# The delta-rule products of the second mixer, issued on the two halves of the array's columns

## What is computed

```python
def gated_delta_rule(q, k, v, g, beta):
    ...
    lower = jnp.where(strict, jnp.einsum("bhnid,bhnjd->bhnij", k_beta, k) * decay, 0.0)
    t_inv = lax.linalg.triangular_solve(eye + lower, ...)
    u = jnp.einsum("bhnij,bhnjd->bhnid", t_inv, v_beta)
    w = jnp.einsum("bhnij,bhnjd->bhnid", t_inv, k_beta * jnp.exp(gc)[..., None])
    attn = jnp.where(tril, jnp.einsum("bhnid,bhnjd->bhnij", q, k) * decay, 0.0)
    def step(state, inp):
        v_new = u_i - jnp.einsum("bhcd,bhde->bhce", w_i, state)
        o = (jnp.einsum("bhcd,bhde->bhce", q_i * jnp.exp(g_i)[..., None], state)
             + jnp.einsum("bhij,bhje->bhie", a_i, v_new))
        state = state * jnp.exp(g_last)[..., None, None] + jnp.einsum("bhcd,bhce->bhde", k_dec, v_new)
        return state, o
```

## Time and profile before

| what | value |
|---|---|
| median of 3 runs | 1586.18 us |
| the profiled execution, its own time | 1586.05 us |
| its span in the trace | 1584.2 us |
| PE (matmul) busy | 1531.3 us, 97% |
| PEld (weight load) busy | 1437.0 us, 91% |
| DVE / ACT / POOL busy | 65% / 53% / 22% |
| DMA | 254.2 MB, mean 160 GB/s |

### The profile page before, as it was taken

One profiled execution on the slowest core, in us unless ns is written; L12 is line 12 of the kernel. 1 busy time (PEld: TensorE's weight loads), 2 busy tenths in 40 slices (PEclk: granted clock), 3 DMA queues, 4 the chain that ended last, 5 costly groups with the idle time before them and its releaser, 6 DMA issues.

```text
span 1584.2 us, 28579 instructions
## 1 busy us (share of the span) xinstructions
PE 1531.3 (97%) x11138; PEld 1437.0 (91%) x11138; DVE 1028.0 (65%) x1792; ACT 836.2 (53%) x1638; POOL 351.3 (22%) x403
## 2 busy tenths in 40 slices
PE   7799999999988989999999999999999999999998
PEld 6389999999988989999999999999999888888886
DVE  4255567555576875476999976777775555555554
ACT  4166455444456543445444457777775554545454
POOL 1133431000155463321465540001112000000000
PEclk9899999999998999999999999999999999999999
DMA  9732455555433442356445554444444656666664
GB/s 216 224 107 81 133 184 169 178 183 186 160 108 113 146 139 77 106 168 195 147 159 174 174 184 151 146 136 145 137 144 162 196 191 196 189 197 194 192 196 137
DMA packets 76771, 254.20 MB, mean 160 GB/s; under 512 B 11375, under 2 KB 15293, under 8 KB 76509
## 3 DMA queue, kind: packets, MB, share of 16 engines
q1 hardware_dynamic: 76397, 251.71, 49.9%
q0 software_dynamic: 240, 0.66, 0.2%
HBM read 250.23 MB, written 1.84 MB: 159 GB/s over the span
## 4 chain that ended last, share of the span: by engine, by line
PE 80%; DVE 12%; DMA 2%; ACT 2%; POOL 2%; issue 1%; SPq 1%; POOLq 0%; DVEq 0%; ACTq 0%
PE bank L675 78%; DVE wl L1661 4%; DVE big L1661 2%; POOL big L2341 2%; DMA big<-in_w1k 1%; ACT big L1236 1%; DVE big L1664 1%; ACT wh L1236 1%; DVE big L2187 1%; DVE big L2198 1%; DVE big L2194 1%; DVE big L2183 1%; DVE big L2204 1%; DVE big L2191 1%; PE bank L984 1%
## 5 line engine op out<-in xcount | busy, mean ns | idle before, releaser
L1661 DVE TENSOR_TENSOR wl<-raw,wh 128x1024 fp32r<-128x1024 f32 (+4 forms) x459 | 531.5, 1159 | 399.5 <-ACT wh L1236 398.9
L1236 ACT ACTIVATE wh<-raw 128x1024 fp32r<-128x1024 f32 (+1 forms) x459 | 482.2, 1053 | 351.3 <-PE bank L675 333.1
L675 PE MATMUL bank<-gw,wh 128*128 128x256 f32 x3504 | 651.3, 287 | 2.4 <-DVE big L1664 2.4
L675 PEld LDWEIGHTS bank<-gw,wh 128*128 128x128 f32 x3504 | 547.4, 193 | 3.0 <-DVE big L1664 2.8
L675 PE MATMUL bank<-gw,wl 128*128 128x256 f32 x1752 | 497.7, 284 | 6.4 <-POOL wl L2341 5.0
L675 PEld LDWEIGHTS bank<-gw,wl 128*128 128x128 f32 x1752 | 336.8, 192 | 8.0 <-issue 6.3
L675 PE MATMUL bank<-xw,wh 128*128 128x256 f32 x1696 | 321.9, 290 | 9.9 <-ACT wh L1236 7.5
L675 PE MATMUL bank<-wh,xw 128*128 128x512 f32 x1056 | 326.9, 391 | 0.0
L675 PEld LDWEIGHTS bank<-xw,wh 128*128 128x128 f32 x1696 | 267.9, 194 | 16.8 <-ACT wh L1236 7.8
L1236 ACT ACTIVATE big<-bank 128x256 f32<-128x256 f32 (+23 forms) x326 | 118.5, 373 | 260.6 <-PE bank L675 222.7
L2341 POOL TENSOR_TENSOR wl<-raw,wh 128x384 fp32r<-128x384 f32 (+3 forms) x131 | 175.6, 1346 | 336.9 <-ACT wh L1236 336.9
(11 more groups left out here) (136 smaller groups left out, 1107.7 us busy)
## 6 DMA issues: line engine op xcount, KB each, us to landing
raw<-in_wst SPq DMA_DIRECT2D x455, 512.0 KB, 3.6
big<-toeplitz SPq DMA_DIRECT2D x8, 256.0 KB, 14.2
big<-in_w1k SPq DMA_DIRECT2D x4, 512.0 KB, 18.1
big<-in_w1v SPq DMA_DIRECT2D x4, 512.0 KB, 19.4
big<-in_xT SPq DMA_DIRECT2D x4, 256.0 KB, 5.0
raw<-in_wst SPq DMA_DIRECT2D x4, 256.0 KB, 4.7
big<-in_keys SPq DMA_DIRECT2D x1, 1024.0 KB, 5.5
out<-big SPq DMA_DIRECT2D x4, 256.0 KB, 2.4
```

Source lines behind the costliest of these rows:

```text
L675: return e.matmul(o, a, b, start=first, stop=last, skip_group_check=True)
L1236: return e.activation(o, x, f, **kw)
L1661: return e.tensor_tensor(o, a, b, f)
```

## The change

A helper `columns` issues a product as two: first columns 0 to 63 of the stationary operand into partitions 0 to 63 of the bank, then columns 64 to 127 into partitions 64 to 127. Both have the same moving operand in full. It takes the place of `mm` in the 54 quads named above. The waits, the semaphore's increment (with the last product of the quad), the banks, the order of the quads and everything on the other engines stay as they are.

```diff
                 def mm(o, a, b, first=True, last=True):
                     return e.matmul(o, a, b, start=first, stop=last, skip_group_check=True)
 
+                def columns(o, a, b):
+
+                    for r in (slice(0, 64), slice(64, 128)):
+                        z = mm(o[r, :], a[:, r], b)
+                    return z
+
...
                         for j in range(4):
                             h, t = 2 * i + j // 2, half(j % 2)
-                            z = mm(b[:, half(j)], K[:, h, t], KB[:, h, t])
+                            z = columns(b[:, half(j)], K[:, h, t], KB[:, h, t])
...
                         for j in range(4):
-                            z = mm(b[:, half(j)], VB[:, 4 * i + j, :], T0[:, 4 * i + j, :])
+                            z = columns(b[:, half(j)], VB[:, 4 * i + j, :], T0[:, 4 * i + j, :])
...
                             m = 4 * i + j
-                            z = mm(b[:, half(j)], TT[:, m, :], YS[:, m, :]) if w == 0 else mm(
+                            z = columns(b[:, half(j)], TT[:, m, :], YS[:, m, :]) if w == 0 else columns(
                                 b[:, half(j)], YS[:, m, :], TT[:, m, :])
```

More of the change, by code:

```diff
@@ L1098, in four @@
                             h, t = 2 * i + j // 2, half(j % 2)
-                            z = mm(b[:, half(j)], K[:, h, t], Q[:, h, t])
+                            z = columns(b[:, half(j)], K[:, h, t], Q[:, h, t])
                     elif what == "y":
@@ L1121, in four @@
                             m = 2 * (4 * i + j)
-                            z = mm(b[:, half(j)], TT[:, m, :], VB[:, m, :])
+                            z = columns(b[:, half(j)], TT[:, m, :], VB[:, m, :])
                     elif what == "s":
@@ L1126, in four @@
                         for j in range(4):
-                            z = mm(b[:, half(j)], KD[:, 4 * i + j, :], VN[:, 2 * (4 * i + j), :])
+                            z = columns(b[:, half(j)], KD[:, 4 * i + j, :], VN[:, 2 * (4 * i + j), :])
                     elif what == "o0":
@@ L1131, in four @@
                             m = 2 * (4 * i + j)
-                            z = mm(b[:, half(j)], DC[:, m, :], VN[:, m, :])
+                            z = columns(b[:, half(j)], DC[:, m, :], VN[:, m, :])
                     elif what == "w":
@@ L1135, in four @@
                         for j in range(4):
-                            z = mm(b[:, half(j)], K[:, 4 * i + j, 128:256], T0[:, 4 * i + j, :])
+                            z = columns(b[:, half(j)], K[:, 4 * i + j, 128:256], T0[:, 4 * i + j, :])
                     elif what == "q":
                         for j in range(4):
-                            z = mm(b[:, half(j)], Q[:, 4 * i + j, 128:256], T0[:, 4 * i + j, :])
+                            z = columns(b[:, half(j)], Q[:, 4 * i + j, 128:256], T0[:, 4 * i + j, :])
                     elif what == "v1":
```

## The result

The changed kernel took 1603.65 us (median of 4 runs, 1600.45 to 1606.39), the kernel before beside it 1586.49. The ratio is 1.0112, with a 95% interval of 1.010 to 1.0124: slower by 17.2 us. Run again later it took 1602.13 us against 1586.42, 15.7 more, ratio 1.0107 (1.009 to 1.0124). The forecast was 1601.5, in a range of 1597 to 1623.

A forecast was written before the change was run, and what follows sets the result against it. PE was taken to bound the kernel on the chain, save beside the inversion. 46 visits at 0.33 us (15.2), 0.2 and -0.02 gave +15.4 on 1586.05, 1601.4; with the runs' median 0.13 higher, 1601.5, range 1597 to 1623.

The forecast's parts named there:

- What bounds: From 588 to 669 us PE is the chain and busy throughout, so every nanosecond it gets or loses is the kernel's.
- Behind the wait: After PE's wait for DVE ends at 588.03 us: 42 visits at 0.33 us, 0.2 for the first quad, -0.02 for a pair.
- The pace: In each changed quad, halves run two at a time: 8 steps of 0.108 to 0.109 us, 0.87 us against 0.89 now.
- The way there and back: At both edges of a changed quad, switching array tile empties the array and exposes a weight load: 0.35 us a visit.
- What I costed at nothing: Six quads beside the inversion: 2.0 us more PE work, hidden in PE's 4.0 us of waits for DVE.
- the `kk` quads: First 4 changed quads, ahead of the inversion and on the chain, at 0.33 us more each.
- the sum: Whole kernel: 46 visits at 0.33 us, 0.2 and -0.02 for two other quads, +15.4 us in all.
- the price per visit: Per changed quad standing alone: 0.87 + 0.35 = 1.22 us instead of 0.89, so 0.33 us more.

## Why the prediction was right

*What bounds.* PE from 588 to 669 us is the chain, and the added work came out at the end: right. Behind the wait 13.5 us were added, against 14.0 forecast (42 x 0.33 + 0.2 - 0.02).

*The pace.* Halves pair up as the row tiles do, and a pair takes the step of a whole product: shown by the sixteen records in 0.82 us, by the half left out, which saved 0.01 us a visit, and by the same half twice, which cost 59 us.

*The way there and back.* Taken as 0.35 us from 30 columns and from 64 rows. From wl to wl the median visit is 1.576 us long, against 1.250, so 0.326 us more where 0.33 was forecast. Less 0.358 for the unit's own products it takes 1.218 us, and less 8 steps of 0.109 that leaves 0.345. What the array does in that time is not shown; the price is. With one product in halves it is the same, with two apart it is paid twice. The Trainium skill's rule on the mode change (TensorEngine Tiling (Array Packing), Key Properties) agrees with this: a price is paid at every change, and it has the size above. Its other rule, that weight loads overlap matmuls in flight only when the row group differs (TensorE: Matmul & The Clock Gate, Part 3, The mechanism), doesn't hold as it stands: only the first of a quad's loads lay open, 0.05 us. The same section also lets a load go ahead when it targets the background weight buffer, and no record here tells whether that is what happened.

*What I costed at nothing.* The six quads beside the inversion: shown, 0.3 us and not to be told from none. I had expected their waits to go from 4.0 to about 2 us in the changed kernel; they went to 3.2. Two things were off. The six quads add 1.6 us there, not 2.0, as two of them stand behind a wait. And DVE's release came 0.7 us later, counted from the end of the `kk` quads: 4.0 - 1.6 + 0.7 is 3.1, and 3.2 was read. The forecast had said that no wait of the other engines gets longer. But the way of the diagonal blocks through DRAM, which lies on the chain, took 0.7 us longer in both profiles of the changed kernel.

*How near the sum is, and by what luck.* The second profile is 15.15 us longer than the one of before: 0.4 us less ahead of the first changed quad, 1.3 for the `kk` quads, 0.7 in the way of the diagonal blocks and 13.5 behind the wait. The forecast had 1.3 and 14.0 and nothing for the others. So the price per visit is right within 0.005 us, but that the whole comes within 0.3 us of 15.4 is in part luck, since two misses of 0.5 and 0.7 us and a scatter of 0.4 cancel for the most part.

*What stays open.* The medians moved by 15.7 and 17.2 us. The runs of the changed kernel spread over 1600.45 to 1606.39 us, so the first is not to be told from 15.4, and the second is 1.8 above it. What comes and goes between executions is of that size: the stretch at the lower clock behind PE's wait, 1.5 us in the profile that has it, and what lies ahead of the change. Of the ten profiles whose program is the same up to 512 us, one comes there 0.5 us before the kernel before and one 2.9 us after it. That these make up the difference was not shown.

## What to carry to other kernels

Cutting a product along the columns of its stationary operand gains nothing where the moving operand is the bound: both halves stream all of it, and the pair takes the time of the whole. And each stay in another tile shape between full-width products costs a third of a microsecond here, whether one cut product is in it or four; so look for narrow products that stand alone between wide ones, and give them the full width, even if most of the result is thrown away. A trace shows it without an experiment: measure from a product ahead of the visit to the same one behind it, and take off the steps.

## What the runs showed of the hardware that I had not expected

- A half on the other tile may start ahead of three waiting records of its neighbour, with their loads, but with seven ahead of it it waits until three are left: 11.5 steps from the first record to the last instead of 7. The order in which tiles are fed need not alternate product by product. Two float32 products of one tile ahead of their partners cost 0.05 us a visit here, four cost 0.48; three were not tried.
- Behind a wait for DVE of 2.1 to 2.3 us the granted clock went to 0.50 for 3.4 us in five profiles of eight and stayed at 1.00 in three, with whole and with cut products alike. It costs 1.5 us where it happens. It is not bound to a wait: in the profile of the two products apart, where TensorE waits for nothing from 534 to 640 us, such a stretch begins at 636.2 us.
- Reading 128 instead of 30 stationary columns costs the stream nothing: four products of 256 elements take four steps of 0.216 us either way.
